# A decoder layer with routed experts: router product in column groups, fewer fillers, and a first gather in halves

## What is computed

```python
def moe_ffn(x2d, w_r, b_r, w1, b1, w2, b2):
    logits = (x2d @ w_r + b_r).astype(jnp.float32)      # (320, 32)
    top_v, top_e = lax.top_k(logits, TOP_K)             # 4 of 32, ties go to the lower index
    gate = jax.nn.softmax(top_v, axis=-1)
    ...
    def expert_block(args):                             # the tokens that chose expert e
        xb, e = args
        h = xb @ w1[e] + b1[e]                          # w1[e]: 1024 x 2048
        g = jnp.minimum(h[:, :D_FF], SWIGLU_LIMIT)
        lin = jnp.clip(h[:, D_FF:], -SWIGLU_LIMIT, SWIGLU_LIMIT)
        act = g * jax.nn.sigmoid(SWIGLU_ALPHA * g) * (lin + 1.0)
        return act @ w2[e] + b2[e]                      # w2[e]: 1024 x 1024
    ...
    return y[:T]                                        # sum of the four outputs, weighted by gate
```

## Time and profile before

| what | us |
|---|---|
| timed runs | 1316.29, 1318.47, 1318.55 |
| median of the three | 1318.47 |
| profiled execution, its own time | 1316.69 |
| its span | 1314.9 |
| busy in the span: TensorE products / VectorE / ScalarE / GpSimd | 1249.4 / 403.2 / 276.0 / 210.1 |
| moved by the transfers | 464.82 MB, 353 GB/s on average |
| expert loads (176 to `big`, 16 to `spare`) | 2048 KB each, 23.0 and 24.4 us from issue to landing |

### The profile page before, as it was taken

How to read it: one execution, slowest core, us unless ns; L and a number is a source line. 1 busy time by engine, 2 the same in 40 slices (tenths; PEclk the granted TensorE clock), 3 DMA queues, 4 the chain that set the end, 5 groups by cost and what they waited for, 6 DMA issues and landing times.

```text
span 1314.9 us, 16064 instructions
## 1 busy us (share of the span) xinstructions
PE 1249.4 (95%) x6478; PEld 649.8 (49%) x6478; DVE 403.2 (31%) x748; ACT 276.0 (21%) x460; POOL 210.1 (16%) x92
## 2 busy tenths in 40 slices
PE   7999999999999999999999999999999999999995
PEld 7989889998953333333333333333333233333332
DVE  3553482375851121202112121212112131211215
ACT  3434443333331010111101011111101011110102
POOL 5665167765400000000000000000000000000000
PEclk9999999999999999999999999999999999999998
DMA  9553675745759999999999999999999999999992
GB/s 317 188 169 136 213 235 176 216 135 189 270 238 427 427 428 429 429 427 430 429 427 429 429 428 429 428 429 429 428 428 429 429 429 428 429 429 427 428 430 93
DMA packets 76955, 464.82 MB, mean 353 GB/s; under 512 B 5137, under 2 KB 43589, under 8 KB 52240
## 3 DMA queue, kind: packets, MB, share of 16 engines
q1 hardware_dynamic: 75328, 459.18, 85.6%
q0 software_dynamic: 1520, 5.12, 1.2%
q10 hardware_dynamic: 72, 0.03, 0.0%
HBM read 461.52 MB, written 2.90 MB: 353 GB/s over the span
## 4 chain that ended last, share of the span: by engine, by line
PE 71%; DMA 23%; DVE 2%; ACT 2%; POOL 1%; issue 1%; SPq 0%; DVEq 0%; ACTq 0%
PE ps L1728 25%; DMA big<-in_w 22%; PE ps L1381 16%; PE ps L1771 11%; PE ps L1687 5%; PE ps L1363 4%; PE ps L1392 2%; PE ps L1673 2%; POOL ring_lo L549 1%; PE ps L1468 1%; PE ps L1487 1%; PE ps L1744 1%; PE ps L1680 1%; ACT w_hi L628 1%; PE ps L1751 1%
## 5 line engine op out<-in xcount | busy, mean ns | idle before, releaser
L1728 PE MATMUL ps<-big,xg 128*64 128x512 f32 x2048 | 466.7, 597 | 28.6 <-DMA big<-in_w 28.3
L1728 PEld LDWEIGHTS ps<-big,xg 128*64 128x64 f32 x2048 | 138.2, 136 | 323.0 <-issue 253.0
L549 POOL TENSOR_TENSOR ring_lo<-ring,w_hi 128x2048 fp32r<-128x2048 f32 x39 | 186.4, 4788 | 111.6 <-ACT w_hi L628 111.5
L1771 PE MATMUL ps<-big,actT 128*64 128x512 f32 x768 | 171.0, 594 | 2.1
L601 POOL TENSOR_TENSOR yacc<-yacc,ln 128x512 f32<-128x512 f32 x1 | 1.6, 1647 | 947.8 <-ACT yacc L836 947.8
L798 ACT ACTIVATE sg<-gm 128x512 f32<-128x512 f32 x32 | 20.2, 631 | 541.7 <-DVE gm L1263 541.7
L1263 DVE TENSOR_SCALAR gm<-ps 128x512 f32<-128x512 f32 x32 | 22.1, 691 | 317.6 <-PE ps L1728 317.6
L1771 PEld LDWEIGHTS ps<-big,actT 128*64 128x64 f32 x768 | 53.0, 136 | 104.7 <-issue 91.8
L1233 DVE TENSOR_TENSOR yacc<-ps,yacc 128x512 f32<-128x512 f32 x75 | 51.9, 691 | 151.0 <-PE ps L1687 142.6
L1224 DVE COPY ypair<-ps 64x512 f32<-64x512 f32 x32 | 22.2, 693 | 236.0 <-PE ps L1771 236.0
L628 ACT CAST w_hi<-ring 128x2048 fp32r<-128x2048 f32 x39 | 74.0, 1901 | 44.0 <-PE ps L1381 28.6
(11 more groups left out here) (295 smaller groups left out, 1125.1 us busy)
## 6 DMA issues: line engine op xcount, KB each, us to landing
big<-in_w SPq DMA_DIRECT2D x176, 2048.0 KB, 23.0
spare<-in_w SPq DMA_DIRECT2D x16, 2048.0 KB, 24.4
ring<-in_w_in SPq DMA_DIRECT2D x24, 1024.0 KB, 5.7
ring<-in_cache_mem_k SPq DMA_DIRECT2D x4, 1024.0 KB, 5.3
ring<-in_cache_mem_v SPq DMA_DIRECT2D x4, 1024.0 KB, 6.3
ring<-in_w_a_out SPq DMA_DIRECT2D x4, 1024.0 KB, 9.8
ring<-in_w_o SPq DMA_DIRECT2D x4, 1024.0 KB, 5.0
ring<-in_w_mk SPq DMA_DIRECT2D x2, 1024.0 KB, 5.2
```

The lines of the kernel that those rows point to most:

```text
L549: pool.tensor_tensor(ring_lo[:, SLOTS[key] % HR, :], slot(*key), w_hi[:, SPLITS.index(key) % 2, :].bitcast(F32), ALU.subtract)\
L1728: ins = pe.matmul(ps[CAP * hh:CAP * hh + CAP, b, :], xg[:, k, par, :], big[:, w1_big, SLOT * kk + 512 * p:SLOT * kk + 512 * p + 512], star ...
L1771: ins = pe.matmul(ps[CAP * dh:CAP * dh + CAP, YB, :], actT[:, kk, j, :], w[:, kk, 512 * dh:512 * dh + 512], start=False, stop=(j == 1 and ...
```

## The change

**Router.** Instead of eight products for each tile with the transposed x as weights, the router's weights (32 columns) are loaded and the transposed x streams through. Steps k, k+4 go to column group k % 4, that is to 32 of 128 PSUM rows, so that four partial sums stand above one another (`quad`). Tiles 2 and 0 are one product of 192 columns, tile 1 is one of 128. VectorE copies the sums to `quads`, and one product of each tile with `quad_sum` (four identity matrices above one another) adds the four parts and turns the result back to tokens. GpSimd makes `quad_sum` at the start.

**Order.** All transposes of x come ahead of the router products; ScalarE rounds tile 0 ahead of its copies, and copies tile 2 after the norm of tile 1. GpSimd forms the low part of tiles 2 and 0; VectorE forms that of tile 1 in two halves, one between mask and ranks, one after the picks. The difference to the largest logit (`ge`) is formed later too.

**Fillers.** None ahead of tile 2's logits, five for nine ahead of the ranks, two for five ahead of the gather.

**Choice.** The scan starts from the count of larger logits instead of zero, so one scalar step falls away; compare and multiply are one instruction.

**First gather.** Half 0 is gathered; then comes the bias product, the turn of half 0, the gather of half 1, and the turn of half 1 after step 0 of the first expert. ScalarE scales half 0 before it copies half 1.

```diff
     t += [("rb", 0)] + [("wo",) + x for x in TOKEN_ORDER]
-    t += [("x1T", 2, 0), ("x1T", 2, 1), ("x1T", 0, 0), ("x1T", 0, 1), ("rt", 2)]
-    return t + [("x1T", 1, 0), ("x1T", 1, 1), ("rt", 0), ("rt", 1), ("rank", 0)]
+    t += [("x1T", tt, h) for tt in TILE_ORDER for h in range(2)]
+    return t + [("quad", 0), ("quad", 1), ("rt", 2), ("rt", 0), ("rt", 1), ("rank", 0)]
...
+            link(pool.memset(quad_sum[:, :], 0.0))
+            for j in range(4):
+                ins = select(quad_sum[:, :], ALU.not_equal, 1.0, -NE * j, [[-1, NE]], 1)
...
-            pool.wait_ge(x_halved, 1)
             pool.wait_ge(*full(*last_use("wo", 3)))
-            pool.tensor_tensor(x_lo[0:64, 2, :], x[0:64, 2, :], x_hi[0:64, 2, :].bitcast(F32), ALU.subtract)\
-                .then_inc(x_split, 1)
+            for tt in (2, 0):
+                r = slice(0, ROWS[tt])
+                pool.wait_ge(x_halved, TILE_ORDER.index(tt) + 1)
+                pool.tensor_tensor(x_lo[r, tt, :], x[r, tt, :], x_hi[r, tt, :].bitcast(F32), ALU.subtract)\
+                    .then_inc(x_split, 1)
...
             for h in range(2):
                 rows_gathered(0, h)
-            for h in range(2):
                 gathered(0, h)
...
+            for h in range(2):
+                dve.wait_ge(*full("quad", h))
+                dve.tensor_copy(quads[:, QUAD_COLS[h]], bank("quad", h)[:, 0:QUAD_COLS[h].stop - QUAD_COLS[h].start])\
+                   .then_inc(*frees("quad", h))
             dve.wait_ge(*copied("rb", 0))
             for tt in TILE_ORDER:
                 r = slice(0, ROWS[tt])
-                if tt < 2:
-                    dve.wait_ge(x_halved, TILE_ORDER.index(tt) + 1)
-                    dve.tensor_tensor(x_lo[r, tt, :], x[r, tt, :], x_hi[r, tt, :].bitcast(F32), ALU.subtract)\
-                       .then_inc(x_split, 1)
...
-            dve.tensor_scalar(nsel[:, :], nsel[:, :], -1.0, float(TOPK), ALU.mult, ALU.add)
             for tt in range(3):
-                ins = dve.tensor_tensor_scan(ceq[:, tt, :], eq[:, tt, :], zeros32[:, :], 0.0, ALU.add, ALU.add)
+                ins = dve.tensor_tensor_scan(ceq[:, tt, :], eq[:, tt, :], zeros32[:, :], nsel[:, tt:tt + 1],
+                                             ALU.add, ALU.add)
             link(ins)
-            link(dve.tensor_tensor(ceq[:, :, :], ceq[:, :, :], nsel[:, :].unsqueeze(2).broadcast_to([P, 3, NE]),
-                                   ALU.is_le))
-            link(dve.tensor_tensor(eq[:, :, :], eq[:, :, :], ceq[:, :, :], ALU.mult))
+            link(dve.scalar_tensor_tensor(out=eq[:, :, :], in0=ceq[:, :, :], scalar=float(TOPK), in1=eq[:, :, :],
+                                          op0=ALU.is_le, op1=ALU.mult))
...
+            dve.wait_ge(x_halved, 3)
+            last_lower(0)
             dve.wait_ge(mask_ready, 1)
...
+            for part, tiles in enumerate(((2, 0), (1,))):
+                cols = QUAD_COLS[part]
+                out = opens("quad", part)
...
+                for k in range(KD):
+                    j = NE * (k % 4)
+                    ins = pe.matmul(out[j:j + NE, 0:cols.stop - cols.start], wr_g[:, k, :], x1T[:, k, cols],
+                                    start=(k < 4), stop=(k >= 4))
+                ins.then_inc(*fills("quad", part))
+            pe.wait_ge(quad_sum_ready, 1)
+            for tt in TILE_ORDER:
+                out = opens("rt", tt)
+                pe.wait_ge(*copied("quad", 1 if tt == 1 else 0))
+                pe.matmul(out[0:ROWS[tt], 0:NE], quads[:, ROUTER_COL[tt]:ROUTER_COL[tt] + ROWS[tt]], quad_sum[:, :],
+                          start=True, stop=True).then_inc(*fills("rt", tt))
             out = opens("rank", 0)
-            keep_clock(out, 9)
+            keep_clock(out, 5)
...
+                        if par == 0 and first and k == 0:
+                            gather_turn(0, 1)
...
-            keep_clock(ps[:, XG, :], 5)
-            pe.wait_ge(x_split, 3)
-            for h in range(2):
-                gather_rows(0, h)
-            for h in range(2):
-                gather_turn(0, h)
+            keep_clock(ps[:, XG, :], 2)
+            pe.wait_ge(x_split, 2)
+            pe.wait_ge(last_split, 1)
+            gather_rows(0, 0)
             pe.wait_ge(ebias_ready, 1)
             up_bias(0, 0)
+            gather_turn(0, 0)
+            pe.wait_ge(last_split, 2)
+            gather_rows(0, 1)
             pair(0, 0, first=True)
```

More of the change, by code:

```diff
@@ L54 @@
 TILE_ORDER = (2, 0, 1)
+ROUTER_COL = {2: 0, 0: 64, 1: 192}
+QUAD_COLS = [slice(0, 192), slice(192, T)]
 def head_slots():
@@ L401, in turned @@
             m = ROWS[tt]
-            copy(x1T[:, 4 * h:4 * h + 4, P * tt:P * tt + m],
+            copy(x1T[:, 4 * h:4 * h + 4, ROUTER_COL[tt]:ROUTER_COL[tt] + m],
                  bank("x1T", tt, h)[:, 0:4 * m].rearrange("p (k t) -> p k t", k=4)).then_inc(*frees("x1T", tt, h))
@@ L768, in _ @@
             normal_right(5, x, 0, x1_right)
-            for h in range(2):
-                act.wait_ge(*full("x1T", 2, h))
-                turned(act.copy, 2, h)
+            halve(0)
             root(6, 1)
             normal_right(6, x, 1, x1_right)
-            halve(0)
-            act.wait_ge(*full("x1T", 1, 1))
-            turned(act.copy, 1, 1)
+            for tt, h in ((2, 0), (2, 1), (1, 1)):
+                act.wait_ge(*full("x1T", tt, h))
+                turned(act.copy, tt, h)
             halve(1)
@@ L1624, in keep_clock @@
                     pe.matmul(out[:, 0:P], ident[:, :], ident[:, :], start=True, stop=True)
-            for key in [key for key in TILES if key[0] in ("x1T", "rt")]:
-                tt = key[1]
+            for tt in TILE_ORDER:
                 m, nth = ROWS[tt], TILE_ORDER.index(tt) + 1
-                out = opens(*key)
-                if key[0] == "x1T":
-                    pe.wait_ge((x1_left, x1_right)[key[2]], nth)
+                for h in range(2):
+                    out = opens("x1T", tt, h)
+                    pe.wait_ge((x1_left, x1_right)[h], nth)
                     for k in range(4):
-                        c = HALF * key[2] + 2 * P * (k // 2)
+                        c = HALF * h + 2 * P * (k // 2)
                         every_other = x[0:m, tt, c:c + 2 * P].rearrange("s (p k) -> s k p", k=2)[:, k % 2, :]
                         ins = pe.transpose(out[:, m * k:m * k + m], every_other, ident[0:m, 0:m])
-                else:
-                    if tt == 2:
-                        keep_clock(out, 4)
+                    ins.then_inc(*fills("x1T", tt, h))
+            for part, tiles in enumerate(((2, 0), (1,))):
+                cols = QUAD_COLS[part]
+                out = opens("quad", part)
+                for tt in tiles:
                     for h in range(2):
                         pe.wait_ge(*copied("x1T", tt, h))
-                    ins = contract(out[0:m, 0:NE], [(x1T[:, k, P * tt:P * tt + m], wr_g[:, k, :]) for k in range(KD)])
-                ins.then_inc(*fills(*key))
+                for k in range(KD):
[4 more added lines that the diff above has]
+            pe.wait_ge(quad_sum_ready, 1)
+            for tt in TILE_ORDER:
+                out = opens("rt", tt)
+                pe.wait_ge(*copied("quad", 1 if tt == 1 else 0))
+                pe.matmul(out[0:ROWS[tt], 0:NE], quads[:, ROUTER_COL[tt]:ROUTER_COL[tt] + ROWS[tt]], quad_sum[:, :],
+                          start=True, stop=True).then_inc(*fills("rt", tt))
             out = opens("rank", 0)
-            keep_clock(out, 9)
+            keep_clock(out, 5)
             pe.wait_ge(mask_ready, 1)
```

24 lines of the change are left out of this document (17 added, 7 removed).

## The result

| | before | changed |
|---|---|---|
| median | 1317.88 (20 runs, 1314.09 to 1320.89) | 1321.91 (20 runs, 1318.42 to 1325.30) |
| profiled execution, own time | 1316.69 | 1324.62 |
| its span | 1314.9 | 1322.8 |
| F, the first load behind the stop | 378.53 | 384.87 |
| first clamp of expert 0, behind F | 10.37 | 12.11 |

The changed kernel is slower: ratio 1.0031, 95% interval 1.0020 to 1.0043. The forecast was 1314.5 in 1312.3 to 1317.9, so sign and range are both wrong.

A forecast was written before the change was run, and what follows sets the result against it. The end stands a fixed distance behind the first load after the stop, set by the TensorE, VectorE and ScalarE chain; gains 2.3 + 0.3 + 0.6 + 0.5 + 0.1 = 3.8, less 0.8 clock, gave 3.0: 1317.5 to 1314.5, range 1312.3 to 1317.9.

The forecast's parts named there:

- The POOL engine takes over tile 0's low part; it has no other work there: Router step: GpSimd forms tile 0's low part, result wanted only by the gather; no cost counted.
- The rival that it stays low up to F: Rival: low clock lasts through gather, turns and first expert products until the first load behind the stop; 1322, chance 0.10.
- the thin stretch: Router to gather, 359.2 to about 365.1, seven fillers for fourteen; clock falls at 362.5, lasts to 366; 0.8 lost.
- the rival of the early fall: Rival: with four fillers gone, clock falls before 357.9 and quad products take 1.2 longer; 1315.7, chance 0.06.
- the gather keeps TensorE as busy as the fillers did: Argument at the first gather against the clock staying low until the first load behind the stop.
- the bounds that I gave, nothing to 1.7: Clock term over ranks, gather and turns: loss between nothing and 1.7, taken as 0.8.
- The reserve of the stream: Expert 0's loads: reserve of 1.8 or a little more before the transfer stream runs dry.
- 1.6 costs nothing: Expert 0's first clamp some 1.6 late, within the stream's reserve of 1.8; no loss counted.
- the rival of the dry stream: Rival: expert 0 lags and the load stream runs dry; with 3 late, 1.2 lost, 1315.7; chance 0.11.
- the router and the choice: Ahead of the ranks: router gains 2.3, choice starting at 361.0; choice of four gains 0.3, mask ready at 362.85.
- the quad products: Router products in four column groups side by side: 0.72 and 0.48, together 1.2; 4.8 if in turn.
- The halves: First gather in halves: 0.8 earlier, less 0.69 for the second turn; net gain 0.1.

The follow-up runs named there:

- e1: Changed kernel, GpSimd starting tile 0's low part only after VectorE normalised tile 1's left half; ratio 1.0004 to the kernel before.
- e4: Kernel before, with tile 0's low part moved to GpSimd and ScalarE's order changed to suit; ratio 1.0018.
- e2: Changed kernel with four, nine and five fillers, the four ahead of tile 1's transposes; ratio 1.0015 to the kernel before.
- e3: Changed kernel with GpSimd's late start on tile 0's low part and four, nine and five fillers; ratio 0.9986 to the kernel before.
- e9: Changed kernel measured again, no edit; ratio 1.0046 to the kernel before.
- e10: Changed kernel with the softmax's exponent moved ahead of ScalarE's scalings, same code as e7 on another chip; ratio 1.0033 to the kernel before.
- e7: Changed kernel with the softmax's exponent moved ahead of ScalarE's scalings, alone; ratio 1.0030 to the kernel before.
- e12: Changed kernel with four, nine and five fillers and the softmax's exponent moved earlier, GpSimd's early start kept; ratio 0.9998 to the kernel before.
- e11: Changed kernel with GpSimd's late start on tile 0's low part and the softmax's exponent moved earlier, seven fillers kept; ratio 0.9982 to the kernel before.
- e5: Changed kernel with GpSimd's late start, four, nine and five fillers, and the softmax's exponent moved earlier; ratio 0.9975 to the kernel before.
- C: Edit to the changed kernel: logit difference formed right behind the mask, softmax's exponent ahead of ScalarE's scalings; alone 1.0030 and 1.0033 to the kernel before.
- e6: Kernel before with only the first gather in halves, bias and turn between them, second turn inside the expert; ratio 1.0000.

## Why the prediction was wrong

**The step that failed first** is the last sentence on the router: "The POOL engine takes over tile 0's low part; it has no other work there". It was costed at nothing because GpSimd was free and the result is wanted late. Both were true. What I did not ask is what the engine blocks while it works: VectorE's normalisation of tile 1, on the chain, for 3.04 instead of 0.80. e1 (0.72) and e4 (3.04 in the kernel before) show it; it costs 2.3 by e2 against e3. The sign of it stood in the trace of before, as 0.80 where its twin for tile 0 took 0.54. The Trainium skill, "SBUF — State Buffer", Who interferes with whom, counts VectorE's `tensor_scalar` among the operations that can get in GpSimd's way. The trace agrees (3.04), and by that rule the step would have had a rival.

**The clock: mechanism named, chance too small.** The rival that it stays low up to F had 0.10 and a price of 1322. Its reason was right (the fillers that lift the clock are removed), its trigger was not in my view: 2.93 in which TensorE stood still. I had put the start of the thin stretch at 359.2 and the fall at 362.5 for 3.5; it fell at 358.3 for 23.9. The profiles tie the early fall to the hole that the stall leaves in TensorE's work: in the changed kernel, e9 and e10 it begins in the hole, in e7 0.7 behind the end of the normalisation; with four fillers in the hole (e2, e12) or without the stall (e1, e11) the clock doesn't fall within 9 us behind H. The transposes alone (the rival of the early fall, 0.06) did not bring it, for e1 and e11 have them without any fillers.

My argument against the rival, that the gather keeps TensorE as busy as the fillers did, is refuted by the windows after: in 371.0 to 378.5 TensorE is busy in all 7.50 and stays at 0.50. e1, without the stall, still has 10.2 of it, and from choice to F 3.1 more than e5, which has none; so the bounds that I gave, nothing to 1.7, were too narrow by themselves. The Trainium skill, "TensorE: Matmul & The Clock Gate", Part 1: The HAM clock gate, has the low clock as the default state and says that activity releases it; the rows agree with the first, while 7.50 of a busy TensorE in 371.0 to 378.5 did not release it. That the median met 1322 is partly luck, since 1.6 of the loss lies elsewhere.

**The reserve of the stream.** I had the clamp 1.6 late; it is 1.74 (12.11 against 10.37). "1.6 costs nothing" was wrong all the same. Timeline of the changed kernel: VectorE waiting for the exponent, its clamp, TensorE waiting for what follows the clamp, and the fifth load, to be read against the earlier trace rows:

```profile
386.04 0.26 DVE L1307 TENSOR_TENSOR ge<-ge,mask 128x96 f32<-128x96 f32 x1 [14.51 <-ACT ge L823]
...
396.98 0.69 DVE L1278 TENSOR_SCALAR gm<-ps 128x512 f32<-128x512 f32 x1
...
399.18 1.13 PE L1776 MATMUL ps<-ident,act_s 128*128 128x128 f32 x4 [2.21 <-DVE act_s L1283]
...
405.67 0.33 SPq L445 DMA_DIRECT2D big<-in_w  x1
```

VectorE stands 14.51 for the exponent, TensorE 2.21 behind the clamp. Then the clock falls once more and the products run at half speed, as the windows have it; the last of them has the hole in the stream:

```profile
399.40:402.60 3.20, 3.20 (x12) 1.26 (x13) 0.00 (x0) 0.60 (x1) 0.00 (x0) 0.50 0.99 425
406.60:407.80 1.20, 1.20 (x8) 0.42 (x6) 0.00 (x0) 0.00 (x0) 0.00 (x0) 1.00 1.25 273
```

The fifth load stands 20.80 behind F, where it stood 17.84. So it is 3.0 late, 1.8 of it free and 1.2 not, and the end moved by 1.56: the rival of the dry stream (chance 0.11, "with 3 late" a loss of 1.2) came true as well, as a second loss beside the clock's. The stream's rule was right; the clock's fall behind a wait was missing in it. With C the fifth load is at 17.8 again.

**What was right.** Apart from the stall, the router and the choice came out as worked out: the choice starts 6.9 behind H in e1, e3 and e5 (predicted 361.0, that is 7.0 behind 353.98), and the mask is ready at 8.9 (predicted 8.9). The ranks follow the mask at once (367.89 and 367.94 in the chain after). Two terms were a little off: the quad products took 1.43 for 1.2, and the scans with a start from memory lie above my bound of 0.15, with 0.64 for three where they took 0.45, which leaves about 0.2 of the 0.3 for the choice:

```profile
366.66 0.64 DVE L1193 TENSOR_TENSOR_SCAN ceq<-eq,nsel,zeros 128x32 f32<-128x32 f32 x3
```

The halves brought 0.2 for 0.1 (e6). The sum of these steps is seen in e11, where the two faults of order are mended: H to F is 2.7 shorter than before (predicted 3.0, with a fall of 3.5 in the clock; it had one of 3.4), and the ratio is 0.9982 (0.9970 to 0.9995), where the forecast was 1314.5/1317.5 = 0.9977. So the costed steps hold in sum, by one profile and one ratio. The ones costed at nothing decided the sign.

**What stays open.** Why the clock falls for 3.4 in one profile, for 10 or 24 in another of nearly the same code, or not at all, is not settled; e7 and e10 are the same code. Shown is that the stall with seven fillers gave a long fall in each of four profiles (13.7 to 23.9), and the mended order with seven fillers a shorter one in both of its two (10.2 and 3.4). What the eleven fillers are worth without the stall stays open too: 1.0004 (e1) against 0.9986 (e3) on one chip, but 0.9982 (e11) against 0.9975 (e5) with the softmax moved, on two chips.

## What to carry to other kernels

An engine that is free is not free of charge: before work is moved onto GpSimd, look up which VectorE instructions from SBUF to SBUF lie in its time, and look for pairs of like instructions of which one is longer in the trace and ends just behind a GpSimd one. When fillers are taken out of a chain, cost the chain at the lower clock from the first wait on, and count a late step not only by its own lateness but with the clock that the wait behind it may cost. A reserve of transfers is spent by the sum of both.

## What was not expected of the hardware

VectorE's instruction did not get its turn between GpSimd's two. Alone, the first takes 2.36, so it ended near 357.1; VectorE's had started at 356.64 and still ended 0.29 behind the second. So two instructions in a row on GpSimd held VectorE up for both. Work of VectorE out of PSUM ran at its normal length beside GpSimd: in e1 three copies of 512 columns took 1.87 while GpSimd was at its 2.38.

The scatter of the runs follows the granted clock. In 35 runs of the kernel before (beside e1 to e4), the mean clock of an execution lies between 0.987 and 0.995 and the span between 1312.6 and 1318.9, with a tendency of the longer ones to the lower clock. Taking the lower level's time as twice the missing share of the span, a run has 18.4 us of it in the median, and along a straight line through the runs each microsecond costs about 0.23 of span. The changed kernel has 40.9, in 20 runs, and 0.19 each: 22.5 us more of it at 0.19 to 0.23 is 4.3 to 5.2, an estimate of the size of the whole loss of 4.0, though not one that separates the stall from it. Worked out in the same way, as an estimate over the whole span, the median run of e7, e9 and e10 has 36 to 44 us, of e1 33, of e2 29, of e12 24 and of e11 18, against 18 to 24 in the three series of the kernel before. These figures count falls elsewhere too (in the profile of before some 10 of 14 lie behind 1304), so they bear out the long fall with the stall without placing it; that e1 has 15 more than e11, from which it differs by the softmax alone, is not explained.
